# The clamped decays of the state-space scan move from VectorE to ScalarE, the masked products and the eight-head matmul burst change place

## What is computed

```
a_cs  = cumsum(dt * a)                                  # per head, 64 heads
decay = exp(segsum(adt))                                # exp(cs[l] - cs[s]) for l >= s, else 0
cb    = einsum('bclgn,bcsgn->bgcls', cc, bc)            # one 256 x 256 matrix per group
y     = einsum('bgcls,bgrcls,bcsgrp->bclgrp', cb, decay, xdt)
y     = y + d_skip * xs
yg    = y * silu(z);  yg = yg * rsqrt(mean(yg*yg) + eps) * norm_g;  out = yg @ w_out
```

## Time and profile before

| | us |
|---|---|
| median of three runs (lowest, highest) | 2419.42 (2419.29, 2419.97) |
| the profiled execution, its time | 2418.89 |
| the profiled execution, its span | 2417.6 |
| TensorE busy in it | 2408.4 |
| VectorE busy | 1570.7 |
| ScalarE busy | 1242.9 |
| granted TensorE clock, mean | 0.999 of 2.4 GHz |

### The profile page before, as it was taken

How to read it: one execution, slowest core, us unless ns; L and a number is a source line. 1 busy time by engine, 2 the same in 40 slices (tenths; PEclk the granted TensorE clock), 3 DMA queues, 4 the chain that set the end, 5 groups by cost and what they waited for, 6 DMA issues and landing times.

```text
span 2417.6 us, 45321 instructions
## 1 busy us (share of the span) xinstructions
PE 2408.4 (100%) x19562; PEld 2333.0 (96%) x19562; DVE 1570.7 (65%) x2105; ACT 1242.9 (51%) x1427; POOL 88.7 (4%) x68
## 2 busy tenths in 40 slices
PE   9999999999999999999999999999999999999998
PEld 9999999999999999999988899999999999999998
DVE  7778888865577776665575556556555555555556
ACT  5446665654364565644464445445444445455463
POOL 0001000100031000000000000000000000000002
PEclk9999999999999999999999999999999999999999
DMA  7766666667755655547767666666655676656645
GB/s 250 209 187 195 200 187 192 183 192 251 237 158 161 190 167 152 155 157 244 220 192 240 197 195 198 190 187 194 186 188 188 191 240 201 183 172 173 191 158 183
DMA packets 263400, 467.37 MB, mean 193 GB/s; under 512 B 16480, under 2 KB 66208, under 8 KB 261280
## 3 DMA queue, kind: packets, MB, share of 16 engines
q1 hardware_dynamic: 263056, 464.21, 62.4%
q10 hardware_dynamic: 144, 0.26, 0.0%
HBM read 451.64 MB, written 4.26 MB: 189 GB/s over the span
## 4 chain that ended last, share of the span: by engine, by line
PE 99%; DVE 0%; DMA 0%; ACT 0%; issue 0%; SPq 0%; ACTq 0%
PE G L675 93%; PE M L675 5%; PE M L688 1%; DMA RAW<-in_ssd_w_in 0%; DVE W1m L1532 0%; DVE TT L2241 0%; DVE RES L2236 0%; ACT W L1102 0%; ACT QKB L1323 0%; DVE RES L2268 0%; ACT PXB L1332 0%; DVE PXB L1967 0%; SPq L555 0%; SPq L543 0%; DVE RES L2271 0%
## 5 line engine op out<-in xcount | busy, mean ns | idle before, releaser
L675 PE MATMUL G<-AA,W 128*128 128x256 f32 x7852 | 930.3, 277 | 0.7 <-ACT W L1102 0.4
L675 PEld LDWEIGHTS G<-AA,W 128*128 128x128 f32 x7852 | 908.2, 188 | 5.7 <-issue 4.0
L1532 DVE TENSOR_TENSOR W<-RAW,W 128x1024 fp32r<-128x1024 f32 (+1 forms) x442 | 553.7, 1255 | 356.5 <-ACT W L1102 355.3
L1102 ACT CAST W<-RAW 128x1024 fp32r<-128x1024 f32 (+1 forms) x442 | 460.4, 1047 | 449.8 <-PE G L675 435.3
L675 PE MATMUL G<-AA,WY 128*128 128x256 f32 x2548 | 308.3, 277 | 0.0
L675 PEld LDWEIGHTS G<-AA,WY 128*128 128x128 f32 x2548 | 297.4, 188 | 1.5 <-issue 1.2
L1532 DVE TENSOR_TENSOR WY<-RAW,WY 128x1024 fp32r<-128x1024 f32 (+1 forms) x114 | 141.8, 1246 | 73.3 <-ACT WY L1102 73.3
L675 PE MATMUL G<-W2m,YY 128*128 128x256 f32 x1512 | 183.5, 276 | 0.0
L675 PE MATMUL G<-W,YY 128*128 128x512 f32 x792 | 181.3, 389 | 0.0
L675 PE MATMUL G<-W1m,YY 128*128 128x256 f32 x1488 | 180.2, 276 | 0.0
L675 PE MATMUL G<-W0m,YY 128*128 128x256 f32 x1488 | 180.2, 276 | 0.0
(11 more groups left out here) (308 smaller groups left out, 2394.4 us busy)
## 6 DMA issues: line engine op xcount, KB each, us to landing
RAW<-in_a_w_in SPq DMA_DIRECT2D x192, 512.0 KB, 3.9
RAW<-in_ssd_w_in SPq DMA_DIRECT2D x160, 512.0 KB, 4.4
RAW<-in_b_w_in SPq DMA_DIRECT2D x128, 512.0 KB, 4.0
RAW<-in_dsa_w_in SPq DMA_DIRECT2D x72, 512.0 KB, 3.7
RAW<-in_ssd_w_out SPq DMA_DIRECT2D x64, 512.0 KB, 4.8
RAW<-in_dsa_w_out SPq DMA_DIRECT2D x64, 512.0 KB, 4.5
RAW<-in_a_w_out SPq DMA_DIRECT2D x64, 512.0 KB, 3.7
RAW<-in_b_w_out SPq DMA_DIRECT2D x32, 512.0 KB, 3.7
```

The lines of the kernel that those rows point to most:

```text
L675: return e.matmul(o, l, r, start=start, stop=stop, skip_group_check=True)
L1102: e.copy(wh[:, 0:n], RAW[:, v % NR, 0:n]).then_inc(*up(cast_done, "cast", v))
L1532: e.tensor_tensor(wl[:, 0:n], RAW[:, v % NR, 0:n], wh[:, 0:n].bitcast(F), ALU.subtract).then_inc(*up(rest_done, "rest", v))
```

## The change

The two `tensor_scalar` of each head leave VectorE. In their place ScalarE computes relu(cs[s] - cs[l]), with scale -1 and the bias from `csT` (now with its sign kept), and the exponential gets scale -1. They stand at ScalarE's units 8 to 11, two heads at a time; the two exponentials stand at 9 and 11. VectorE has the masked products at units 8 and 11, `XD` at 9 and 10. TensorE has one burst of all eight heads at unit 16. SyncE has the `CSB` DMA at unit 5. `gate_z` starts one unit later. The pieces of the diff stand in this order: the walk, SyncE, TensorE, ScalarE, VectorE.

```
-            run(("z", g), later(0 if g == 0 else 2, "gate_z", g))
+            run(("z", g), later(1 if g == 0 else 3, "gate_z", g))
...
         def ssd(g):
-            for _ in range(6):
+            for _ in range(5):
...
             yield
+            yield
+            e.wait_ge(*on("read", "xd", g, 1))
             for i in range(2):
                 b = take("ty", g, i)
-                if i == 0:
-                    e.wait_ge(*on("read", "xd", g, 1))
                 e.wait_ge(*on("em", g, i))
...
-                yield
-                yield
+            yield
...
-            yield
+            e.wait_ge(*on("cs", g))
+            e.wait_ge(*on("csT"))
+            if g > 0:
+                e.wait_ge(*on("y_m", g - 1, 3))
             for i in range(2):
+                for h in range(4 * i, 4 * i + 4):
+                    hh = 8 * g + h
+                    if h % 4 == 2:
+                        yield
+                    e.activation(E2[:, h, 0:256], CSB[:, h, :], ACT.Relu, scale=-1.0,
+                                 bias=csT[:, 0, hh:hh + 1]).then_inc(*up(act_made, "decay", g, i))
+                    e.activation(E2[:, h, 256:384], CSB[:, h, P:T], ACT.Relu, scale=-1.0,
+                                 bias=csT[:, 1, hh:hh + 1]).then_inc(*up(act_made, "decay", g, i))
                 ev = E2[:, 4 * i:4 * i + 4, :].rearrange("p h n -> p (h n)")
                 e.wait_ge(*on("decay", g, i))
-                e.activation(ev, ev, ACT.Exp).then_inc(*up(act_made, "ee", g, i))
-                for _ in range(4):
-                    yield
+                e.activation(ev, ev, ACT.Exp, scale=-1.0).then_inc(*up(act_made, "ee", g, i))
+                yield
...
-        def decay(g, i):
+        def masked(g, i):
+            e.wait_ge(*on("ee", g, i))
+            if i == 0:
+                e.wait_ge(*on("read", "cb", g))
+            e.tensor_tensor(E2[:, 4 * i:4 * i + 4, :], E2[:, 4 * i:4 * i + 4, :],
+                            CB[:, :].unsqueeze(1).to_broadcast([P, 4, 384]), ALU.mult).then_inc(
+                                *up(dve_made, "em", g, i))
...
             yield
-            yield
-            e.wait_ge(*on("cs", g))
-            if g > 0:
-                e.wait_ge(*on("y_m", g - 1, 3))
-            decay(g, 0)
+            masked(g, 0)
             yield
...
+            masked(g, 1)
+            for _ in range(4):
+                yield
```

More of the change, by code:

```diff
@@ L1606, in dt_task @@
             e.tensor_copy(dtT[:, :, :], m[:, 0, :, 0:64]).then_inc(*up(dve_made, "dtT"))
-            e.tensor_scalar(csT[:, :, :], m[:, 1, :, 0:64], -1.0, None, ALU.mult).then_inc(*up(dve_made, "csT"))
+            e.tensor_copy(csT[:, :, :], m[:, 1, :, 0:64]).then_inc(*up(dve_made, "csT"))
             here(dve_made, "read", "dtT")
             yield
-        def decay(g, i):
[L1612 to L1617, removed]
+        def masked(g, i):
[5 more added lines that the diff above has]
+                                *up(dve_made, "em", g, i))
         def ssd(g):
@@ L1650, in ssd @@
                 yield
[L1651 to L1657, removed]
+            masked(g, 1)
+            for _ in range(4):
                 yield
-                if i == 0:
-                    decay(g, 1)
-                    yield
             for q in range(4):
```

## The result

| | us |
|---|---|
| the changed kernel, median of four runs (lowest, highest) | 2451.68 (2445.70, 2455.05) |
| the kernel before, median of four runs | 2419.51 |
| ratio, 95% interval | 1.0131 (1.0120 to 1.0143) |
| profiled execution: time, span | 2445.70, 2444.4 |
| its TensorE, VectorE, ScalarE busy | 2413.8, 1543.8, 1275.9 |

The change makes the kernel 32 us slower, 1.3%. The times scatter over 9 us, where those of before lie within 0.7. I forecast 2438.4, with the right direction and mechanism and 13 us too little. The median lies above my forecast of 2431 to 2449 and only 0.3 us under 2452, the end of my range; one of the four executions took 2455.05.

The account below looks back on a forecast made before the run. Bound taken: the number and pace of TensorE's matmuls. 2418.89 + 15.6 (stops, groups 1 to 6) + 5.3 (group 7) - 1.9 (burst borders) = 2437.9 us, 2438.4 for the median; range 2421 to 2452.

Parts of the forecast that it names:

- The bound: TensorE, busy 2408.4 of 2417.6 us: only its pace where its order changes and new weight waits can move the time.
- The relus: On ScalarE, 0.49 and 0.40 us each, 0.69 us a head with overlap, 5.6 us a group.
- The order and the stops: ScalarE and VectorE wait on each other; unit 16's weights late by 2.6 us in groups 1 to 6, 15.6 in all.
- Group 0: No gate ahead of it, so the chain ends some 3 us earlier; counted as 0.
- Group 7: One buffer fewer, each rest needed a unit sooner: stops of 1.0, 0.7, 0.1 and 3.5 us, together 5.3.
- Two of the waits that I named: New waits: ScalarE ahead of L1158 for `CSB`, 0.8 us; VectorE ahead of L1624 for ScalarE, 5 us a group.
- The borders: TensorE: one burst in place of two saves 0.24 us of borders, 8 times, -1.9 us.
- 2418.89 + 15.6 + 5.3 - 1.9: Profiled time before, stops in groups 1 to 6, stops in group 7, border gain: 2437.9 us for the profiled execution.
- dearer relus or a late `CSB`: Rival of longer stops: relus at 0.89 us a head give 2449, `CSB` 2 us later 2452; 12 in 100 over 2449.
- The page of the table load: Chain's three table loads on ScalarE: 1.28 us each; about 1.38 of drain more would make an estimated 2460; forecast without drain.
- The rule for relu: Rows agreed with keeping relu on VectorE: 0.46 us a head against 0.69 on ScalarE, speaking against the change.

Follow-up runs that it names:

- one_burst: The kernel before with only TensorE's edit, one burst of eight heads behind unit 16 instead of two of four: 2420.17 us.
- half_relus: The changed kernel with the decays of heads 4 to 7 back on VectorE, right ahead of the first masked product: 2421.66 us.
- mask_later: The changed kernel with the first masked product one step later on VectorE, at unit 9: 2419.67 us.
- both_moves: The changed kernel with the first masked product at VectorE's unit 9 and the `CSB` DMA at SyncE's unit 4: 2415.32 us.
- filled_ten: The changed kernel with 10 unread matmuls on TensorE in each of groups 1 to 7, ahead of the weight wait: 2442.20 us.
- order_dve: both_moves with all eight decays of a group on VectorE in one piece at unit 8, no relus on ScalarE: 2415.32 us.
- csb_earlier: The changed kernel with the `CSB` DMA one fetch earlier still, at unit 4: 2429.28 us.
- filled: The changed kernel with 18 unread matmuls on TensorE in each of groups 1 to 7, ahead of the weight wait: 2447.26 us.

## Why the prediction was right, and where it was short

**The bound.** Right. TensorE's pace and its waits explain the runs: what its waits and its busy time gained or lost gives the change of the span within 0.1 us for the changed kernel, and within 0.2 for the others but one_burst, where 0.5 us are missing.

**The relus.** Right. 500 and 387 ns in the trace of after (0.49 and 0.40 taken), 0.70 us a head; half_relus shows that their time counts only inside the chain.

**The order and the stops.** Right, shown by mask_later. 3.16 us measured in group 1 against 2.6, mostly since `CSB` landed at 193.2 and not at 192.5; 2.2 in groups 2 and 5, where `CSB` held ScalarE for 1.0 us and not for 1.9 to 2.7 as in the others. Group 0 has no stop, as forecast. Group 7 has stops of 1.5, 0.3 and 3.2 against my 1.0, 0.7, 0.1 and 3.5. The sum was 20.9, the trace has 21.9. Two of the waits that I named were too short, 0.8 us ahead of L1158 (2.24 in group 1) and 5 us a group on VectorE ahead of L1624 (69.5 in all, 8.7 a group); the second costs TensorE nothing.

**The borders.** Right in sign, too small: I had 1.9 us; both_moves shows TensorE busy for 3.9 us less than before. In the changed kernel that gain is there too, and hidden under what follows.

**The step that failed** is the sum itself: "2418.89 + 15.6 + 5.3 - 1.9" counts a stop as the time that TensorE stands still and nothing behind it. The runs showed a second price: the granted clock falls behind some of the stops, in the first profile behind those of groups 1, 4 and 6 (3.1 to 3.2 us) and not behind those of 2 and 5 (2.2 us), of 3 (3.12 us) and of 7 (3.16 us), and the unit behind takes 4.4 to 5.4 us instead of 3.0. My sum has TensorE's busy time fall by 1.9 us; it rose by 5.4 in one execution and by 11.6 in the other. That is 7.3 and 13.5 us that the sum lacks; the waits are 0.6 and 2.3 us more than I had. Together 7.9 and 15.8, and the two executions took 2445.70 and 2453.56, 7.8 and 15.7 over the sum's 2437.9.

Those 7.3 and 13.5 us are not all clock. The slow units and the bursts behind them hold 4.7 us in the first execution and 12.1 in the other. The 0.3 us that each of nine stops costs beside its length make some 2.9, and 2.0 go off since the borders and the merged bursts gave 3.9 and not 1.9. That leaves 1.7 and 0.5 us that I cannot place. The clock's part differs by 7.4 us between the two executions, and they lie 7.9 us apart: it is most of the scatter. filled_ten, where the stops stay and the clock does not fall, bears this out: its span is 27.1 us over that of both_moves, which are its 23.6 us of stops and 3.5 more, 0.3 for each of the eleven. Its 2442.2 is 3.8 us over my 2438.4, with no fall of the clock in it.

**The range held by luck.** The median stands in the band over 2449, to which I had given 12 in 100 for dearer relus or a late `CSB`. Neither brought it there: a head's relus took 0.70 us and not 0.89, and `CSB` was 0.7 us late in group 1. What did was the price behind the stops, which stands nowhere in my prediction.

**The page of the table load.** The loads in the chain take 1.28 us, and the `SZ<-G` silu follows 0.01 us behind (210.70 + 1.28 to 211.99), so no drain stands behind it either. The trace agrees with the load's price in the Trainium skill ("ScalarE: Activation LUTs", "What ACT_TABLE_LOAD costs") and shows nothing of the 1.38 us of drain beside it, on which my 2460 rested.

**The rule for relu** of the same page of the Trainium skill ("Rules for kernel authors"), to keep it on VectorE, holds in price per head, 0.46 against 0.70 us, and decides nothing in that order: order_dve and both_moves take the same time.

**What stays open.** Why the clock fell behind a stop of 2.24 us and behind most of 3.1 and not behind others of 2.16, 2.50, 3.12 and 3.16, and why the slow stretch is longer in some executions. I tried nothing that sets the moment of a stop. Nor was it tried whether group 7's remaining 3.1 us of csb_earlier have a cause of their own; both_moves removes them.

## What to carry to other kernels

In a program where every engine runs strictly in order, place an instruction by when its input is ready on the other engine, not by where a step is free: a product put one step ahead of its exponential made two engines wait for each other and cost 32 us in this kernel, and one step later it cost nothing. Write down, for each instruction that waits, everything queued behind it and who waits for that, two hops far; then compare the chain's length with the lead of the resource behind it. And where TensorE is the bound, count a stop at its length and some 0.3 us at its borders, and 1.5 to 2.7 us more where the granted clock falls behind it, which here it did behind stops of 2.24 us and more, not behind all of them, and behind none shorter.

## What the hardware showed that I had not expected

- Behind a stop of 3.1 us, the next 24 matmuls took 4.56 us in one execution and 5.42 in another, against 2.97 behind another stop of 3.1 us; behind a stop of 2.24 us 4.42, behind one of 2.16 us 2.95. The granted clock of the stretches was 0.76 and 0.72 where it was slow and 1.00 where it was not.
- A stop costs TensorE some 0.3 us beside its length with the clock at its higher level: in group 1 of csb_earlier the units ahead of and behind a stop of 1.04 us take 5.83 us (208.76 to 215.63, less the stop), and 5.54 in both_moves, which does not stop there (208.69 to 214.23).
- Matmuls that nobody needs, put into the wait, made the kernel 9 us faster (2442.2 against 2451.1).
- An f32 matmul of 128 columns against an identity leaves two records and takes 0.22 us (18 of them 3.93 in filled); a transpose of the same size takes one record and 0.09 (four of them 0.36, 197.44 to 197.80 in the trace of before).
- A merged burst of 32 matmul records into two banks took 2.80 us, two of 16 took 1.51 each.
